# A fifth read-ahead buffer for expert weights, in the space reserved for GpSimd's DMA descriptors

## What is computed

```python
for l in range(DEPTH):                      # DEPTH = 2
    h = rmsnorm(x, norm1_g[l])
    # one input projection h @ w_in[l]; forgetting attention (4 heads), dilated attention (4 heads), Mamba-2 SSD
    mix = jnp.concatenate([o_fox, o_dil, o_ssd], axis=-1)
    x = x + mix @ w_out[l]
    h = rmsnorm(x, norm2_g[l]); m = rmsnorm(mem, mem_norm_g[l])
    x = x + memory_cross_attention(h, m, xa_wq[l], xa_wkv[l], xa_qn_g[l], xa_kn_g[l], xa_wo[l])
    h = rmsnorm(x, norm3_g[l])
    x = x + hierarchical_moe(h, ...)        # top-1 of 4 groups, top-2 of 8 experts inside it
# one expert: (silu(xb @ w1[e]) * (xb @ w3[e])) @ w2[e], w1 and w3 1024 x 512, w2 512 x 1024, 32 experts a layer
```

## Time and profile before

| what | value |
|---|---|
| time, median of 3 runs | 1596.47 us |
| lowest and highest | 1595.89 and 1597.43 us |
| span of the profiled execution | 1589.7 us |
| median less span | 6.8 us |
| PE busy | 1185.8 us (75%) |
| ring loads of expert weights | 184 of 2 MB, 23.7 us from issue to landing (median) |
| loads into the four other buffers | 2 of each, one a layer |
| chain that ended last | PE 45%, DMA 42% |

### The profile page before, as it was taken

One profiled execution on the slowest core, in us unless ns is written; L12 is line 12 of the kernel. 1 busy time (PEld: TensorE's weight loads), 2 busy tenths in 40 slices (PEclk: granted clock), 3 DMA queues, 4 the chain that ended last, 5 costly groups with the idle time before them and its releaser, 6 DMA issues.

```text
span 1589.7 us, 16075 instructions
## 1 busy us (share of the span) xinstructions
PE 1185.8 (75%) x6030; PEld 557.3 (35%) x6031; DVE 321.3 (20%) x835; ACT 221.5 (14%) x491; POOL 43.9 (3%) x81
## 2 busy tenths in 40 slices
PE   6999898977656656566579998988776566566565
PEld 4765544442212212112147645445322122122121
DVE  1125613131101101101021256131311011011010
ACT  4124312110000000000031243122000000000000
POOL 0110000000000000000001100000000000000000
PEclk9999999989989889889889999999798889789888
DMA  9563145379999999999974631453799999999997
GB/s 350 159 212 107 54 158 198 120 274 409 409 410 410 410 410 410 410 410 410 371 250 124 212 107 53 159 211 119 276 410 409 410 409 410 409 410 410 409 410 288
DMA packets 143333, 476.65 MB, mean 300 GB/s; under 512 B 6358, under 2 KB 14894, under 8 KB 143278
## 3 DMA queue, kind: packets, MB, share of 16 engines
q1 hardware_dynamic: 141616, 472.62, 77.0%
q10 hardware_dynamic: 1662, 3.32, 0.6%
HBM read 474.87 MB, written 1.05 MB: 299 GB/s over the span
## 4 chain that ended last, share of the span: by engine, by line
PE 45%; DMA 42%; DVE 5%; issue 3%; SPq 2%; ACT 2%; DVEq 0%; ACTq 0%
PE bank L1264 43%; DMA ring<-exp_w 42%; SPq L523 2%; PE bank L1280 2%; DMA ring<-w_in 1%; DVE X L1245 1%; ACT fox_ssd L817 0%; ACT Y L606 0%; DVE proj_ht L1147 0%; DVE fox_ssd L979 0%; ACT SCO L778 0%; DVE smax L1112 0%; ACT H L766 0%; DVE fox_ssd L1051 0%; DVE proj_ht L1029 0%
## 5 line engine op out<-in xcount | busy, mean ns | idle before, releaser
L1264 PE MATMUL bank<-ring,proj_ht 128*32 128x512 f32 (+3 forms) x2432 | 439.7, 650 | 151.9 <-DMA ring<-exp_w 149.7
L1264 PEld LDWEIGHTS bank<-ring,proj_ht 128*32 128x32 f32 (+1 forms) x2432 | 153.3, 133 | 384.1 <-issue 189.8
L1264 PE MATMUL bank<-ring,SCO 128*32 128x512 f32 x1024 | 165.7, 784 | 114.0 <-DMA ring<-exp_w 112.6
L1264 PEld LDWEIGHTS bank<-ring,SCO 128*32 128x32 f32 x1024 | 34.6, 129 | 234.4 <-DMA ring<-exp_w 148.1
L1264 PE MATMUL bank<-ring,conv_mem 128*128 128x512 f32 x256 | 114.6, 601 | 1.1 <-DVE Y L1061 1.1
L1264 PE MATMUL bank<-ring,H 128*128 128x512 f32 x256 | 112.3, 594 | 2.6 <-ACT H L606 1.5
L1245 DVE TENSOR_TENSOR X<-X,bank 128x512 f32<-128x512 f32 x64 | 44.0, 688 | 338.0 <-PE bank L1264 338.0
L1264 PE MATMUL bank<-proj_ht,H 128*128 128x128 f32 x512 | 73.4, 294 | 23.9 <-DVE proj_ht L1147 23.9
L1264 PEld LDWEIGHTS bank<-proj_ht,H 128*128 128x128 f32 x512 | 64.0, 200 | 62.6 <-DVE proj_ht L1147 35.8
L1264 PE MATMUL bank<-fox_ssd,proj_ht 128*128 128x512 f32 (+1 forms) x160 | 62.5, 600 | 20.6 <-ACT fox_ssd L817 20.6
L1264 PEld LDWEIGHTS bank<-ring,H 128*128 128x128 f32 x256 | 47.8, 190 | 59.5 <-issue 59.4
(11 more groups left out here) (189 smaller groups left out, 812.1 us busy)
## 6 DMA issues: line engine op xcount, KB each, us to landing
ring<-exp_w SPq DMA_DIRECT2D x184, 2048.0 KB, 23.7
ring<-w_in SPq DMA_DIRECT2D x8, 2048.0 KB, 17.8
ring<-xa_wkv SPq DMA_DIRECT2D x8, 2048.0 KB, 11.9
ring<-w_out SPq DMA_DIRECT2D x4, 2048.0 KB, 9.8
ring<-xa_wq SPq DMA_DIRECT2D x4, 2048.0 KB, 9.2
ring<-xa_wo SPq DMA_DIRECT2D x4, 2048.0 KB, 7.7
ring<-w_in SPq DMA_DIRECT2D x6, 1024.0 KB, 12.3
conv_mem<-exp_w SPq DMA_DIRECT2D x2, 2048.0 KB, 12.7
```

Source lines behind the costliest of these rows:

```text
L1264: return nc.tensor.matmul(dst, lhsT, rhs, start=start, stop=stop)
```

## The change

The space that the compiler keeps for descriptors of DMAs issued by GpSimd (which issues none here) is given up by an argument of the program's constructor. A new buffer `ahead` of one unit takes it, and becomes the first of five spare buffers. `SPARE_UNITS` becomes 2 to 6: unit 2 goes to `ahead`, 3 to `conv_mem`, 4 to `fox_ssd`, 5 to `keys_values`, 6 to `proj_ht`. With `SHIFT` = 5 the units from 7 on go to slot (n - 5) % 6: 7, 8, 9, 10 to slots 2, 3, 4, 5, and 11 to slot 0. `LAST_IN_SLOT` follows: slots 0 to 5 now hold units 11, 6, 7, 8, 9, 10 last. The load into `ahead` has no wait of its own. The wait of unit 0 of the second quad keeps its count.

```diff
-SPARE_UNITS = (2, 3, 4, 5)
+SPARE_UNITS = (2, 3, 4, 5, 6)
 SHIFT = len(SPARE_UNITS)

-HEAD_ORDER = (0, 1, 6, 7, 2, 3, 4, 8, 9, 5, 10, 11)
+HEAD_ORDER = (2, 0, 1, 7, 8, 3, 4, 5, 9, 10, 6, 11)


 def moe_slot(n, head):

-    if head and n < SLOTS:
-        return None if n in SPARE_UNITS else n
+    if head and n in SPARE_UNITS:
+        return None
+    if head and n < SPARE_UNITS[0]:
+        return n
     return (n - SHIFT) % SLOTS
...
         ring = sb("ring", [P, SLOTS, UNIT])
+        ahead = sb("ahead", [P, UNIT])
...
-        spare = (conv_mem[:, 0:UNIT], fox_ssd[:, 0:UNIT], keys_values[:, :], proj_ht[:, PROJ_HT - UNIT:])
+        spare = (ahead[:, :], conv_mem[:, 0:UNIT], fox_ssd[:, 0:UNIT], keys_values[:, :], proj_ht[:, PROJ_HT - UNIT:])
...
-                            sp.wait_ge(*full((("kv", 3, 1), ("ysT", NT - 1), ("xo", 1, XH - 1), ("router",))[i], l))
-                            alone(sp)
+                            if i:
+                                sp.wait_ge(*full((("kv", 3, 1), ("ysT", NT - 1), ("xo", 1, XH - 1), ("router",))[i - 1], l))
+                                alone(sp)
...
-    nc = bacc.Bacc("TRN2", target_bir_lowering=False, num_devices=1)
+    nc = bacc.Bacc("TRN2", target_bir_lowering=False, num_devices=1, dynamic_dma_scratch_size=128)
```

## The result

The changed kernel takes 1571.51 us (median of 4 runs, 1568.85 to 1573.37) against 1596.18 us for the kernel before (4 runs, 1595.61 to 1597.43). The ratio is 0.9841, with a 95% interval of 0.9824 to 0.9858. That is 24.7 us or 1.6% **faster**, where "no change" with a range of 1593.5 to 1599.0 was predicted. The prediction is wrong. The span of the profiled execution is 1571.5 us, after 1589.7.

The account below looks back on a forecast made before the run. The expert stages were taken as bound by the weight stream at 410 GB/s. All terms were 0, so 1589.7 + 0 + 0 + 0 + 6.8 = 1596.5 us, no change, with a range of 1593.5 to 1599.0.

Parts of the forecast that it names:

- the count of 19: Second quad's unit 0 still waits for unit 6 of the head, so the 84 units start as before: 0 gained.
- The unit saved: End of the head: one unit less to fetch, 5.115 us of transfer, spent in a longer idle hole: 0 per layer.
- The load into `ahead`: Behind the last dense load at 201.23: another 5.1 us of transfer fits and nobody waits for it: 0.
- the turn: Into layer 1: fv waits one unit longer, slips 3.4 us (fqk 1.5) against 13 us of slack: 0.
- The time with "issue" as its reason: PE's 12.04 us before 806.70, which could not be priced: bounded at -3.4 to +3.4, taken as 0.
- Rival B: Fv and the dense loads of layer 1 come late, up to 3.4 us slower: 1599.9 us; chance 0.04.
- Rival C: PE runs the head faster with DMA engines idle: under 0.5 us a layer, counted as no change; no separate chance.
- The freed space: GpSimd issues no DMA, so nothing else changes; 1 us either way for what lies outside the span and moved addresses: 0.
- the signs that the prediction listed: Profile: issues near 337.7 and 351.5, empty DMA about 348 to 352, then 410 GB/s, small fv part near 789.9.
- three signs of being wrong: Second issue before PE's unit 6 ends, PE waiting for DMA inside the head, or PE starting fv after 811.
- Rival A: The stream starts earlier by the unit saved: 4.1 us a layer, 8.2 in all, 1588.3 us; chance 0.07.
- 6.8 us lie outside the span: Time outside the profiled span, 1596.47 - 1589.7, added to the span to give the forecast time.

Follow-up runs that it names:

- e3: The changed kernel with the 128-byte buffer slot_no moved ahead of the ring, which starts 128 over a multiple of 256: 1598.76 us, ratio to the kernel before 1.0007.
- e8: The changed kernel again, timed on one chip beside two other kernels: 1576.28 us, ratio to the kernel before 0.9877.
- e9: The kernel before with 128 unused bytes ahead of the ring, timed on the same chip as e8: 1575.43 us, ratio 0.9872.
- e1: The kernel before with 128 unused bytes ahead of the ring, which then starts at byte 16640: 1576.56 us, ratio 0.9874.
- e5: The kernel before with 160 unused bytes ahead of the ring, which then starts 32 over a multiple of 256: 1597.7 us, ratio 1.0013.
- e6: The kernel before with 96 unused bytes ahead of the ring, which then starts 224 over a multiple of 256: 1597.72 us, ratio 1.0013.
- e4: The changed kernel with the wait of the second quad's unit 0 set to unit 1 of the head: 1570.37 us, ratio to the kernel before 0.9836.
- e10: The kernel of e4 again, timed on the same chip as e8: 1572.63 us, ratio to the kernel before 0.9856.
- e2: The kernel before with the reservation cut from 16384 to 256 bytes, ring at byte 384: 1595.48 us, ratio 1.0.
- e11: The kernel before with the reservation cut to 384 bytes, so that the ring starts at byte 512: 1573.68 us, ratio 0.9848.
- e7: The kernel before with 128 unused bytes behind the ring, which stays at byte 16512: 1596.12 us, ratio 1.0005.

## Why the prediction was wrong

**What held.** The stage is bound by the stream. Its start hangs on "unit 6 used", by the count of 19: seen at 354.38, 13.79 us behind the first issue (13.8 was given). The unit saved went into a hole: e3, and e8 against e9, put its worth at 0. The load into `ahead` delayed nobody. At the turn, the small part of fv waited for unit 11 and went at 782.05, the main part at 782.9, landing 5.9 us later at 788.8; PE came to fv at 802.73, 13.9 us behind, where 13 us of slack were counted. The time with "issue" as its reason, for which -3.4 to +3.4 had been allowed, went from 12.04 to 12.57. Rival B did not occur. Rival C didn't either: units in the head took 1.92 and 1.90, where the rows before have 1.99, 1.92 and 1.90.

**What failed** is one step, *The freed space*: "I allow 1 us either way for it and for moved addresses, and take 0." It was worth -19 to -25 us (e1 and the change). The prediction took the 410 GB/s of the earlier trace rows as what the engines can do, and priced the unit at 5.115 us in both kernels. It was the rate of a misplaced ring. Of the signs that the prediction listed, the schedule's came true (some 3 us late in layer 0, and early behind it) and "410 GB/s from 354 on" did not, and none of its three signs of being wrong occurred: it had none for this. The term should have read: 84 units x (5.115 - 4.975) us x 2 layers = -23.5 us. That the ring moves by 16256 bytes, from 128 over a multiple of 256 onto one, was there to be seen in the diff and in the buffer lists of the two programs; no row of the trace before showed what it would be worth.

The size of the step is seen in the packets: 163.8 ns against 159.0, 3.0% more at 128 over. The theory of a cost by distance gave, as estimates, 160.2 ns at 32 over and 167.4 at 224; the packets of e5 and e6 took 163.6 and 163.9 ns, 2.9% and 3.1% more than 159.0. So the three starts off a multiple of 256 that were tried all cost, and the cost did not grow with the distance. Why it is one step stays open: the second theory of e5, one more transaction at any such start, would fit these three places, but no trace here shows transactions.

**Rival A** was wrong in its place and in its size. Nothing started earlier in the changed kernel; with the wait set right (e4, e10) the start did come earlier, and the last units of the stages began 4.8 and 4.3 us earlier in all, where 8.2 had been worked out.

**The base.** "6.8 us lie outside the span" mixed two executions. In the changed kernel's profiled execution the span is 1571.5 and its own time 1573.37, so 1.9 us lie outside, and in every run on record it is 1.8 to 2.0. The kernel before ran between 1590.8 and 1601.0 us in the later timings; its profiled execution, at 1589.7 + 1.8 = 1591.5 or so, was one of the quick ones. So the two spans differ by 18.2 us where the medians differ by 24.7: the one profile is 4.7 us under its median, the other 1.9 above. A forecast good to 0.2% was not to be had from one span and a median of three.

## What to carry to other kernels

Where a stage is bound by a stream of loads, look at the destination's byte address in the partition as the built program lists it, not only at its size: here 128 unused bytes ahead of the ring, which put it on a multiple of 256, gave the whole gain of a change that also reworked buffers, slots and order. A change of the reservation (e2, e11), or a buffer put ahead (e1, e3), moved the ring here, and this kernel won 1.2 to 1.6% by it with nothing gained from the schedule; a run with the old offset restored (e3) told the two apart. The buffer more was worth nothing as long as the wait that guards the next load counted a use that the slot no longer depended on. And a match of one stage with a forecast to 0.1 us can be chance: look which of its parts moved.

## What the runs showed of the hardware

- The expert loads, 4 KB packets from HBM into the ring in SBUF, ran at 421 to 422 GB/s with the ring at a multiple of 256 bytes in the partition (256, 512 and 16640 were tried), and at 410 GB/s at 32, 128 and 224 over (16672; 16512 and 384; 16608). A packet took 159.0 ns, nearly without spread, in the one case, and 163.6 to 163.9 ns on average, nearly all within 159 to 172, in the other.
- How far over the start was made no difference: 410 GB/s at all three distances (e5, e6, e7).
- TensorE's granted clock made none either: 410 GB/s in a window at 0.75 (e7) and at 0.88 (e5).
- TensorE's clock showed where PE's work ends the stage: in the kernel before, the changed one, e4, e8 and e10 the last unit's 16 matmuls took 1.92 us at a granted clock of 1.00 and 3.24 to 3.38 us at 0.55 to 0.58.
- The size of the reservation, 16384 or 256 bytes, in kernels whose loads are all issued by SyncE and ScalarE, made no difference to these loads with the ring 128 over in both (e2: 410 GB/s, ratio 1.0, 0.9983 to 1.0017).
